# Two heads' scores on two row groups, a later wait for the stored gates, and ScalarE weighing the SSD inputs

## The reference, cut to what matters

```python
# stick-breaking attention, 8 heads x 64
z = einsum("bihd,bjhd->bhij", q, k) * 64**-0.5 + bias
log_keep = where(mask, log_sigmoid(-z), 0)
log_tail = cumsum(log_keep, axis=3, reverse=True) - log_keep
weights = exp(where(mask, log_sigmoid(z) + log_tail, -inf))
out = einsum("bhij,bjhd->bihd", weights, v)

# SSD in chunks of 128 tokens, 16 heads x 64, 2 B/C groups, state 128
xd = xh * dt[..., None];  cs = cumsum(dt * a) in the chunk
y_diag = einsum("bclsg,bclsge,bcsgep->bclgep", cb, decay, xd)
to_end = exp(cs[:, :, -1:] - cs)
chunk_states = einsum("bclgn,bclge,bclgep->bcgepn", bc, to_end, xd)
h = h * chunk_decay + chunk_states          # over the 4 chunks
y = y_diag + einsum("bclgn,bcgepn,bclge->bclgep", cc, h_in, exp(cs))
```

## Time and profile before

| | |
|---|---|
| median of 3 runs | 1459.49 us (1457.28 to 1459.98) |
| the profiled execution | 1456.16 us |
| its span, first to last instruction | 1454.4 us |
| PE busy | 1425.9 us, 98% |
| DVE busy | 799.2 us, 55% |
| ACT busy | 487.2 us, 33% |
| POOL busy | 199.0 us, 14% |
| granted clock of PE over the span | 0.996 |

### The profile page before, as it was taken

The page is one execution under the profiler, slowest core; times in us unless marked ns, Lnnn a source line. Parts: engine busy times, 40 slices in busy tenths (PEclk is TensorE's granted clock), DMA queues, the critical chain, the costliest instruction groups (busy, mean ns, idle before and its releaser), DMA issues.

```text
span 1454.4 us, 28517 instructions
## 1 busy us (share of the span) xinstructions
PE 1425.9 (98%) x11704; PEld 1395.1 (96%) x11704; DVE 799.2 (55%) x983; ACT 487.2 (33%) x651; POOL 199.0 (14%) x195
## 2 busy tenths in 40 slices
PE   8999999999999999999999899999999999999999
PEld 8999999999999999999998788899999999999999
DVE  5444444333346557475887799775556654443222
ACT  5222222222243435352233644543332232222111
POOL 1000000000100000006700021110146750000000
PEclk9999999999999999999999899999999999999999
DMA  6332332333332313329957954565345552333232
GB/s 177 96 93 87 91 97 85 91 117 105 103 109 59 86 45 101 84 57 303 319 180 206 160 151 109 175 185 177 89 131 173 161 156 87 91 94 90 84 92 84
DMA packets 274776, 180.99 MB, mean 124 GB/s; under 512 B 13744, under 2 KB 253584, under 8 KB 274592
## 3 DMA queue, kind: packets, MB, share of 16 engines
q1 hardware_dynamic: 264512, 151.56, 36.9%
q0 software_dynamic: 6752, 22.27, 4.9%
q10 hardware_dynamic: 3456, 6.39, 1.2%
HBM read 162.42 MB, written 17.77 MB: 124 GB/s over the span
## 4 chain that ended last, share of the span: by engine, by line
PE 81%; DVE 10%; ACT 3%; issue 3%; SPq 2%; DMA 1%; DVEq 0%; ACTq 0%
PE ps L458 73%; PE ps L1917 2%; DVE w_lo L437 2%; PE ps L1696 1%; PE ps L1706 1%; PE ps L1712 1%; DMA stage<-in_w_in 1%; ACT w_hi L432 1%; SPq L556 1%; DVE hin L1308 1%; DVE gbuf L1320 1%; PE ps L1723 1%; DVE ysm L1333 1%; DVE csb L1317 1%; DVE state L1332 1%
## 5 line engine op out<-in xcount | busy, mean ns | idle before, releaser
L458 PE MATMUL ps<-xg_hi,w_hi 128*128 128x260 f32 x2512 | 513.8, 286 | 3.5 <-DVE w_lo L437 2.0
L458 PE MATMUL ps<-xg_hi,w_lo 128*128 128x260 f32 x2512 | 506.3, 283 | 0.0
L458 PE MATMUL ps<-xg_lo,w_hi 128*128 128x260 f32 x2512 | 505.7, 283 | 0.0
L437 DVE TENSOR_TENSOR w_lo<-stage,w_hi 128x1024 fp32r<-128x1024 f32 (+1 forms) x229 | 299.3, 1307 | 254.1 <-ACT w_hi L432 249.1
L458 PEld LDWEIGHTS ps<-xg_hi,w_hi 128*128 128x128 f32 x2512 | 388.1, 189 | 9.8 <-issue 5.6
L458 PEld LDWEIGHTS ps<-xg_hi,w_lo 128*128 128x128 f32 x2512 | 387.6, 189 | 0.0
L458 PEld LDWEIGHTS ps<-xg_lo,w_hi 128*128 128x128 f32 x2512 | 387.1, 189 | 0.0
L432 ACT ACTIVATE w_hi<-stage 128x1024 fp32r<-128x1024 f32 (+1 forms) x229 | 237.7, 1038 | 347.6 <-PE ps L458 272.3
L458 PE MATMUL ps<-hid_hi,w_hi 128*128 128x260 f32 x704 | 141.9, 283 | 0.0
L458 PE MATMUL ps<-hid_hi,w_lo 128*128 128x260 f32 x704 | 141.5, 282 | 0.0
L458 PE MATMUL ps<-hid_lo,w_hi 128*128 128x260 f32 x704 | 141.3, 282 | 0.0
(11 more groups left out here) (301 smaller groups left out, 1464.4 us busy)
## 6 DMA issues: line engine op xcount, KB each, us to landing
stage<-in_w_in SPq DMA_DIRECT2D x69, 512.0 KB, 5.0
stage<-in_ffn_w_gate SPq DMA_DIRECT2D x44, 512.0 KB, 3.8
stage<-in_ffn_w_up SPq DMA_DIRECT2D x44, 512.0 KB, 3.8
stage<-in_ffn_w_down SPq DMA_DIRECT2D x32, 448.0 KB, 3.8
stage<-in_ffn_w_down SPq DMA_DIRECT2D x16, 512.0 KB, 4.0
pages<-in_cache_sb_k SPq DMA_DIRECT2D x32, 256.0 KB, 4.5
pages<-in_cache_sb_v SPq DMA_DIRECT2D x32, 256.0 KB, 3.8
gates<-gates_kept POOLq DMA_DIRECT2D x24, 260.0 KB, 4.0
```

The source lines that it names most:

```text
L437: nc.vector.tensor_tensor(low(u0)[:, 0:kt, :], stage[:, s, 0:kt, :], high(u0)[:, 0:kt, :].bitcast(F32), ALU.subtract).then_inc(unit_split, 1)
L458: mm = nc.tensor.matmul(out[:, h, :], wt[:, k, :], v[:, h * HALF:(h + 1) * HALF], start=start and k == 0 and n == 0, stop=stop and k == kt ...
```

## The change

The scores of both heads are made together: for each block of columns the matmul of head 0 (partitions 0 to 63) is followed by that of head 1 (64 to 127), into neighbouring banks. They come in two bursts, first the blocks j = 0 and 1 of both heads (896 columns each), after half of unit 4 the blocks j = 3 and 2 (384 columns). The parts on which ACT and DVE work change from 640 and 640 to 384 and 896 columns. The order of all three engines in the turn is rewritten. In the SSD stage DVE's wait for the stored gates moves behind the head products of tile 0, `xde` is made by ACT in eight scaled copies of 64 columns, ACT also copies the first chunk's state, and DVE makes `xd` of the next tile directly behind the states.

```diff
-SCORE_PARTS = (slice(640, SCORES), slice(0, 640))
+SCORE_PARTS = (slice(896, SCORES), slice(0, 896))
@@ ACT, attention
-                        act.wait_ge(z_biased.sem, z_biased.now(t, 2 * e + n))
+                        act.wait_ge(z_biased.sem, z_biased.now(t, (2 + e, e)[n]))
...
                 softplus_log(0)
-                softplus_high(0)
+                softplus_high(0, 0)
                 round_unit(U_ATT + 6, up, DT)
+                softplus_high(0, 1)
+                softplus_log(1)
                 weights(0)
+                softplus_high(1, 0)
+                softplus_high(1, 1)
                 round_unit(U_ATT + 7, up, DT)
-                softplus_log(1)
-                softplus_high(1)
                 round_unit(U_ATT + 8, up, DT)
                 weights(1)
@@ ACT, SSD
+            def weigh_states(t):
+                act.wait_ge(xd_ready.sem, xd_ready.now(0, t))
+                act.wait_ge(dt_end_made, 1)
+                act.wait_ge(states_ready.sem, states_ready.now(0, t - 1))
+                for c in range(CH):
+                    for e in range(2):
+                        at = P * c + HD * e
+                        last = nc.scalar.activation(xde[:, c, HD * e:HD * e + HD], ps[:, turned_bank(t), at:at + HD],
+                                                    ACT.Copy, scale=dt_end[:, c, 2 * t + e:2 * t + e + 1])
+                last.then_inc(xde_ready.sem, 1)
+
+            def copy_state(t):
+                act.wait_ge(states_ready.sem, states_ready.now(0, t))
+                act.wait_ge(y_summed.sem, y_summed.now(0, t - 1))
+                nc.scalar.activation(hin[:, 1, :], ps[:, 5, 0:P], ACT.Copy).then_inc(first_state, 1)
...
             decays(0, 0)
+            weigh_states(0)
             decays(0, 1)
             for t in range(SSD_T):
...
                     round_unit(u + (1, 3)[t % 2], 0, DT)
+                copy_state(t)
...
                 if t % 2 == 0:
                     round_unit(u + 2, 0, DT)
+                if t < SSD_T - 1:
+                    weigh_states(t + 1)
@@ DVE, attention (part 0: 512 and 384 columns of each head, part 1: 384)
                 take_z(0)
                 bias_z(0)
                 rest_unit(U_ATT + 5, up, DT)
+                bias_z(1)
                 softplus(0)
+                softplus_low(0, 0)
+                rest_unit(U_ATT + 6, up, DT)
+                softplus_low(0, 1)
+                log_beta(0)
+                take_rest(4, zs[:, ds(2 * t + 1, 1), :])
...
                 take_tail(0)
+                softplus(1)
+                softplus_low(1, 0)
+                softplus_low(1, 1)
                 mask_weights(0)
+                take_rest(5, xb[:, ds(3 * t, 1), 3:3 + T])
                 rest_unit(U_ATT + 7, up, DT)
+                log_beta(1)
+                take_rest(6, xb[:, ds(3 * t + 1, 1), 3:3 + T])
                 take_tail(1)
                 rest_unit(U_ATT + 8, up, DT)
                 mask_weights(1)
+                take_rest(7, xb[:, ds(3 * t + 2, 1), 3:3 + T])
@@ DVE, SSD
-                dve.wait_ge(states_ready.sem, states_ready.now(0, t - 1))
-                nc.vector.tensor_tensor(xde[:, :, :].rearrange("p c (h d) -> p c h d", h=2), turned,
...
             nc.vector.memset(hin[:, 0, :], 0.0)
-            gates_stored(dve, GATES - G_POST)
...
                 dve.wait_ge(states_ready.sem, states_ready.now(0, t))
+                dve.wait_ge(first_state, t + 1)
...
-                last = nc.vector.tensor_copy(hin[:, 1, :], ps[:, 5, 0:P])
...
                 tile_states(t)
+                if t < SSD_T - 1:
+                    tile_xd(t + 1)
...
                 head(t, 0)
                 head(t, 1)
+                if t == 0:
+                    gates_stored(dve, GATES - G_POST)
                 if t % 2 == 0:
                     sc_unit(it, 0)
-                if t < SSD_T - 1:
-                    tile_xd(t + 1)
@@ PE, attention
+                def scores(part):
+                    if part == 0:
+                        pe.wait_ge(qk_normed.sem, qk_normed.now(t, 1))
+                    else:
+                        pe.wait_ge(z_biased.sem, z_biased.now(t, 1))
+                    for j, bank, at in (((0, 4, 0), (1, 6, 0)), ((3, 4, 0), (2, 4, 128)))[part]:
+                        for e in range(2):
+                            rows = slice(HD * e, HD * e + HD)
+                            mm = nc.tensor.matmul(ps[:, bank + e, at:at + SCORE_W[j]], kh[rows, P * j:P * j + P],
+                                                  qh[rows, P * j:NP], start=True, stop=True)
+                    mm.then_inc(scored.sem, 1)
...
                 scores(0)
-                unit(4)
+                unit(4, end=4)
+                scores(1)
+                unit(4, begin=4)
...
-                unit(5, end=4)
+                unit(5)
                 tails(0)
-                unit(5, begin=4)
-                scores(1)
                 unit(6)
-                unit(7, end=2)
                 tails(1)
-                unit(7, begin=2)
+                unit(7)
                 values()
@@ PE, SSD: the states wait for xde_ready(t), the y product also for xd_ready(t),
   the transposes of tile t for both of tile t-2
```

More of the change, by code:

```diff
@@ L743, in softplus_log, with softplus_high @@
                                              ).then_inc(log_ready.sem, 1)
-                def softplus_high(e):
-                    for n, part in enumerate(SCORE_PARTS):
-                        act.wait_ge(sp_made.sem, sp_made.now(t, 2 * e + n))
-                        nc.scalar.activation(spl_hi[:, e, part], spl[:, e, part], ACT.Copy
-                                             ).then_inc(sp_hi_ready.sem, 1)
+                def softplus_high(e, n):
+                    part = SCORE_PARTS[n]
+                    act.wait_ge(sp_made.sem, sp_made.now(t, 2 * e + n))
+                    nc.scalar.activation(spl_hi[:, e, part], spl[:, e, part], ACT.Copy).then_inc(sp_hi_ready.sem, 1)
                 def weights(e):
@@ L1056, in take_x, with bias_z @@
                     take(5 + j, xb[:, ds(3 * t + j, 1), 3:3 + T].rearrange("p o (a b) -> p (o a) b", a=2))
-                def bias_z(e):
-                    dve.wait_ge(scored.sem, scored.now(t, e))
-                    for part in SCORE_PARTS:
-                        nc.vector.tensor_scalar(zb[:, e, part], flat[:, 2048 + part.start:2048 + part.stop],
-                                                sb_bias[:, ds(2 * t + e, 1)], None, ALU.add).then_inc(z_biased.sem, 1)
+                def bias_z(part):
+                    dve.wait_ge(scored.sem, scored.now(t, part))
+                    for e in range(2):
+                        bias = sb_bias[:, ds(2 * t + e, 1)]
+                        if part == 0:
+                            nc.vector.tensor_scalar(zb[:, e, 0:512], ps[:, 4 + e, :], bias, None, ALU.add)
+                            nc.vector.tensor_scalar(zb[:, e, 512:896], ps[:, 6 + e, 0:384], bias, None, ALU.add
+                                                    ).then_inc(z_biased.sem, 1)
+                        else:
+                            nc.vector.tensor_scalar(zb[:, e, 896:SCORES], ps[:, 4 + e, 0:384], bias, None, ALU.add
+                                                    ).then_inc(z_biased.sem, 1)
                 def mask_diagonal(buf, part):
@@ L1077, in softplus, with softplus_low, log_beta @@
                         mask_diagonal(spl[:, e, :], n).then_inc(sp_made.sem, 1)
-                    for n, part in enumerate(SCORE_PARTS):
-                        dve.wait_ge(sp_hi_ready.sem, sp_hi_ready.now(t, 2 * e + n))
-                        nc.vector.tensor_tensor(spl_lo[:, e, part], spl[:, e, part], spl_hi[:, e, part].bitcast(F32),
-                                                ALU.subtract).then_inc(sp_ready.sem, 1)
+                def softplus_low(e, n):
+                    part = SCORE_PARTS[n]
+                    dve.wait_ge(sp_hi_ready.sem, sp_hi_ready.now(t, 2 * e + n))
+                    nc.vector.tensor_tensor(spl_lo[:, e, part], spl[:, e, part], spl_hi[:, e, part].bitcast(F32),
+                                            ALU.subtract).then_inc(sp_ready.sem, 1)
+                def log_beta(e):
                     link(nc.vector.scalar_tensor_tensor(zb[:, e, :], zb[:, e, :], 0.0, lg[:, e, :], ALU.min,
@@ L1688, in head_sums, with tails @@
                     mm.then_inc(qk_summed.sem, 1)
-                def scores(e):
-                    pe.wait_ge(qk_normed.sem, qk_normed.now(t, 1))
+                def scores(part):
+                    if part == 0:
+                        pe.wait_ge(qk_normed.sem, qk_normed.now(t, 1))
+                    else:
+                        pe.wait_ge(z_biased.sem, z_biased.now(t, 1))
+                    for j, bank, at in (((0, 4, 0), (1, 6, 0)), ((3, 4, 0), (2, 4, 128)))[part]:
+                        for e in range(2):
+                            rows = slice(HD * e, HD * e + HD)
```

(10 more changed lines are left out.)

32 lines of the change are left out of this document (12 added, 20 removed).

## The result

The kernel after takes 1451.8 us (median of 5 runs, 1449.42 to 1452.48), the kernel before 1459.49 beside it: a ratio of 0.995, 95% interval 0.9935 to 0.9964. The gain is 7.7 us where the forecast had 14.8; the time lies inside the range. The profiled execution took 1451.9 us with a span of 1450.1, that of before 1456.16: a difference of 4.3 only, because that execution of before was 3.3 under its median.

The account below looks back on a forecast made before the run. PE, busy 98% of the span, was taken as the bound; attention's 7.7 us plus SSD's 7.1 gave 14.8 us, so a median of 1444.7 us for 1459.49, range 1439 to 1454.

Parts of the forecast that it names:

- Part 1: Attention scores: both heads' bursts overlap fully on two row groups, 2.6 us a turn for 4.84, gaining 2.2.
- Rival B: Attention scores: row halves take turns, scores and attention waits give 0, only SSD's 7.1 us remains: 1452.4; 9%.
- C: Attention: the DVE and ACT chain sets the turn and eats 1.9 us of it: 1452.4; 8%.
- Part 2: Attention turn's new order: four tail waits of 0.42 us go, five tight meeting points add 0.7 us a turn.
- the 0.7 of new waiting: Attention turn: new waiting assumed from some ten DVE and ACT hand-overs, 0.7 us a turn, bounds 0 and 2.6.
- the bound named as 0: Attention turn: no new waiting if each hand-over goes as in the rows; four turns then give 10.4 us.
- D: Attention: the same chain is 5 us later a turn than walked, kernel 5.2 us slower: 1464.7; 6%.
- The gates wait and the first tile: SSD entry: moved gates wait costs nothing, PE waits 0.7 us for 6.3, y(0) comes 5.7 us earlier.
- The late load: SSD tile 1: unit 3's weights, issued at 812.89, land at 819.6; ACT waits, leaving 2.9 us gained at y(1).
- The steady tiles: Later SSD tiles: 12.4 us even, 12.65 odd against 13.3 and 12.9; last 13.1 for 13.99.
- The clock: SSD waits of about 3 us before y(0) and y(1): a fall is hidden before y(0), costs 2.9 us before y(1).
- rival A: SSD: the clock falls in one of the new waits, 2.6 us back, 1447.3; 10%.

Follow-up runs that it names:

- the bunched stores: Kernel after the change, with SyncE's small stores moved together behind the loads and stores of SSD tiles 0 and 1: 1450.31 us (0.9939).
- both mended orders: Kernel after the change, with GpSimd's additions a tile later and SyncE's small stores spread over tiles 2 to 5: 1447.47 us (0.9932).

## Why the forecast was wrong, step by step

By places in the two profiled executions the forecast's 14.8 us become 4.3 like this: attention +2.65, the fall at 730 us -1.5, up to y(0) -0.7, tile 1 -1.7, y(1) to y(7) -7.4, behind y(7) -1.85.

**Part 1 holds.** A turn's bursts take 1.77 + 0.93 = 2.70 us for the forecast 2.6, so 2.14 gained for 2.2. Rival B is out. That the measured 1451.8 lies next to the 1452.4 of B and C is chance: neither happened.

**Part 2 was too careful.** PE has no wait in the attention turns at all. 10.35 us came, 2.59 a turn: 2.2 + 0.42 without the 0.7 of new waiting. That was the bound named as 0. C and D are out.

**The gates wait and the first tile hold within 0.7 us.** y(0) gained 5.0 us in the stage for 5.7. The eight copies took 1.73 us for 2.1; PE's wait for xde was 1.3 for 0.7.

**The late load was seen and undersized.** Counted from the entry of the stage, SP issued it at 14.1 us for the forecast 13.7, but it took 8.3 us to land and not the 6.7 of the earlier trace rows. The state store behind it on SP wasn't walked at all; DVE waited 4.8 us for it, and by it alone tile 1 would have been late: in the kernel with both copies on DVE, y(0) to y(1) takes 18.5 us behind the same store. After y(1) 0.5 us of the stage's gain were left for the forecast 2.9.

**The steady tiles are the step that failed.** It said 12.4 and 12.65 us a tile and 13.1 for the last; the trace has 13.64, 13.09, 14.35, 14.65, 13.73 and 13.60 from y(1) to y(7), 7.4 us more in all. The walk had PE, ACT and DVE, and left POOL out, that is, it put what POOL's additions cost DVE at nothing without a reason. With the additions a tile later the tiles from y(3) take 12.41, 13.10, 12.72 and 12.49: y(4) and the last are what the walk gave or less, y(6) 0.3 more and the odd y(5) 0.45 more (rounding, state copy, states, products one after the other: y waits 0.99 in tiles 3 and 5 of both kernels). Tiles 2 and 3 stay as they were, 1.7 over the walk; most of it is tile 2's, which runs behind the fall of y(1) and takes 12.37 where the clock stays up. y(1) to y(7) falls from 83.06 us to 77.45, 5.6, and the time by 5.7. That DVE's products can meet POOL's additions stood in the trace of before as the product of 1.77 us at 906.95, just ahead of the 2.33 us before y(7); the forecast passed it over.

**The clock was half right.** That it may fall was named as rival A, at 10% and for one wait. It fell behind three in the stage and once before it; filler in the three waits gave 3.0 us, though only two of their falls went. The forecast's idea that a fall before y(0) is hidden in the wait before y(1) is borne out (y(1) came at the same place with and without it), but y(1)'s and y(4)'s weren't hidden. The price was too high for a fall in this trace: 3.4 us at the lower level and 1.7 lost, not 5.8 and 2.9; in other runs the low stretch was twice as long (803 to 810 us with the bunched stores). The rule cited there (the Trainium skill, "TensorE: Matmul & The Clock Gate", "Why this matters for your kernels") held more often than the earlier trace rows had led to believe.

**The sum by medians:** forecast 14.8 = 7.7 + 7.1; measured 10.7 for the attention, and with the SSD part on top of it 3 to 4 less than that, so it gave nothing of its 7.1. By single edits POOL's place is worth 5.7, of which some 1.5 came through the clock, filler 3.0 and the small stores 1.5 or 2.1, the last not clear of noise; they don't simply add. Left open: 1.85 us that the profiled execution lost behind y(7), where PE's waits for w_lo are 2.4 us for 1.0; and why the runs with both mended orders scatter over 7 us.

## What to carry to other kernels

Walk every engine through a stage whose order shifts, the nearly idle one too: an elementwise operation on POOL that was harmless in one place cost DVE 1.1 us in another. Before you blame an operation that moved, move what it displaced: the state copy's 5.3 us vanished when POOL's additions stood elsewhere. A wait removed brings the next thing in the queue forward, here SP's load and store, so walk that queue as well. And try a new place in the kernel where it is to stand: the later additions gave 5.7 us where DVE had pauses, while in the kernel before, where it has none, they and the spread stores together cost 2.6.

## What the runs showed of the hardware

Two row halves of the array run beside each other: the 1280 columns of each of two heads took 1.77 + 0.93 = 2.70 us together, in two bursts, where 1280 columns of one had taken 2.42. A gate product of 512 columns that starts while GpSimd adds ends 0.54 to 0.56 us behind the addition, and a weight rest or state product of 1024 columns 1.07 to 1.10, in all kernels and whenever it started. Scaled copies of 64 columns on ACT cost 1.73 us for eight, 0.2 each. Filler matmuls made one kernel 7.5 us faster, and another 3, the latter hardly clear of noise. The length of a wait alone doesn't settle whether the clock falls: behind the same wait of 2.33 us before y(7) it stayed up before and fell in the kernel with the attention part and the moved gates wait (898.4 to 901.8 us); behind 1.93 it stayed up before y(7) of the kernel after and fell before y(5) of the one with the state copy on DVE and both orders mended (869.6 to 873.0); behind 2.80 it stayed up in the kernel with both orders mended, and it fell once with no wait at all.
